# A hybrid recurrence, sparse attention and S5 trunk: one-engine steps and a new order between the weight chunks

## The reference

```python
h = rms_norm(x, norm_g) * (1.0 + scale) + shift
proj = h @ w_in
ya = hgrn2_mixer(hg_q, hg_f, hg_i, lb, hg_onorm_g) * jax.nn.silu(hg_g)
yb = dsa_mixer(at_q, at_k, at_v, ix_q, ix_k, ix_w, positions, at_qnorm_g, at_knorm_g) * jax.nn.silu(at_g)
yc = s5_mixer(s5_u, s5_a_re, ..., s5_glu_w, s5_glu_b) * jax.nn.silu(s5_g)
yd = jnp.einsum('bsnw,nwd->bsnd', jnp.stack([ya, yb, yc], axis=2), w_branch)
merged = jnp.einsum('bsnd,bsnd->bsd', jax.nn.sigmoid(merge_g).reshape(B, S, 3, D), yd)
x = x + gate * (merged @ w_out)
```

## Time and profile before

| | |
|---|---|
| time, median of 3 runs | 1408.55 us (1406.85 to 1410.6) |
| the profiled execution | 1403.91 us, span 1402.1 us |
| mean granted clock of TensorE | 0.955 |
| PE, DVE, ACT, POOL busy | 1290.5, 857.0, 501.4, 488.6 us |
| idle time of PE in the span | 111.6 us |
| HBM | 99 GB/s over the span |

### The profile page before, as it was taken

The page is one execution under the profiler, slowest core; times in us unless marked ns, Lnnn a source line. Parts: engine busy times, 40 slices in busy tenths (PEclk is TensorE's granted clock), DMA queues, the critical chain, the costliest instruction groups (busy, mean ns, idle before and its releaser), DMA issues.

```text
span 1402.1 us, 16539 instructions
## 1 busy us (share of the span) xinstructions
PE 1290.5 (92%) x6240; PEld 1039.1 (74%) x6240; DVE 857.0 (61%) x1396; ACT 501.4 (36%) x774; POOL 488.6 (35%) x344
## 2 busy tenths in 40 slices
PE   7899899789997999989989999988899799999997
PEld 4687787666776877878756877866767588888886
DVE  5775595687647745884464656947865576533241
ACT  5253213443325342333232431143425353333331
POOL 1253222333343323644404432322324332245451
PEclk9999999799997999999989999999999989899999
DMA  9332210032122225562435221110411213344322
GB/s 357 129 135 61 60 61 31 15 137 74 61 90 54 76 77 179 190 243 88 160 123 213 90 61 60 58 34 17 149 61 45 90 55 88 84 155 151 97 69 76
DMA packets 64176, 142.05 MB, mean 101 GB/s; under 512 B 31200, under 2 KB 31328, under 8 KB 63328
## 3 DMA queue, kind: packets, MB, share of 16 engines
q1 hardware_dynamic: 63040, 138.89, 30.2%
q10 hardware_dynamic: 1056, 2.10, 0.4%
HBM read 128.12 MB, written 10.49 MB: 99 GB/s over the span
## 4 chain that ended last, share of the span: by engine, by line
PE 64%; DVE 13%; ACT 8%; SPq 5%; DMA 4%; issue 4%; POOL 1%; DVEq 0%; ACTq 0%
PE bank L1665 16%; PE bank L1666 16%; PE bank L1667 16%; PE bank L1852 4%; DMA raw<-in_wfull 3%; SPq L696 2%; SPq L723 2%; PE bank L1837 2%; SPq L687 1%; PE bank L1921 1%; PE bank L1814 1%; PE bank L1677 1%; ACT w_hi L785 1%; DVE ada L1118 1%; PE bank L1824 1%
## 5 line engine op out<-in xcount | busy, mean ns | idle before, releaser
L756 POOL TENSOR_TENSOR w_lo<-raw,w_hi 128x512 fp32r<-128x512 f32 (+1 forms) x170 | 244.1, 1436 | 893.1 <-ACT w_hi L785 893.1
L1665 PE MATMUL bank<-h_hi,w_hi 128*128 128x512 f32 x896 | 366.0, 408 | 2.3 <-POOL w_lo L757 2.3
L1666 PE MATMUL bank<-h_lo,w_hi 128*128 128x512 f32 x896 | 351.7, 393 | 0.0
L1667 PE MATMUL bank<-h_hi,w_lo 128*128 128x512 f32 x896 | 351.5, 392 | 0.0
L785 ACT ACTIVATE w_hi<-raw 128x1024 fp32r<-128x1024 f32 (+2 forms) x170 | 178.9, 1055 | 300.0 <-PE bank L1667 156.5
L757 POOL TENSOR_TENSOR w_lo<-raw,w_hi 128x512 fp32r<-128x512 f32 (+2 forms) x170 | 252.5, 1486 | 0.0
L1665 PEld LDWEIGHTS bank<-h_hi,w_hi 128*128 128x128 f32 x896 | 170.5, 190 | 45.8 <-issue 8.9
L1666 PEld LDWEIGHTS bank<-h_lo,w_hi 128*128 128x128 f32 x896 | 170.2, 190 | 39.7 <-issue 5.5
L1667 PEld LDWEIGHTS bank<-h_hi,w_lo 128*128 128x128 f32 x896 | 169.9, 190 | 36.6
L1665 PE MATMUL bank<-w_hi,h_hi 128*128 128x512 f32 (+1 forms) x256 | 98.8, 386 | 10.1 <-POOL w_lo L757 4.6
L1666 PE MATMUL bank<-w_lo,h_hi 128*128 128x512 f32 (+1 forms) x256 | 96.5, 377 | 0.0
(11 more groups left out here) (275 smaller groups left out, 1826.4 us busy)
## 6 DMA issues: line engine op xcount, KB each, us to landing
raw<-in_wfull SPq DMA_DIRECT2D x178, 512.0 KB, 3.7
arena<-in_wada SPq DMA_DIRECT2D x40, 512.0 KB, 5.4
x_scratch<-xm SPq DMA_DIRECT2D x2, 2048.0 KB, 8.2
arena<-x_scratch SPq DMA_DIRECT2D x2, 2048.0 KB, 9.4
arena<-in_x SPq DMA_DIRECT2D x4, 512.0 KB, 6.0
arena<-in_s5m SPq DMA_DIRECT2D x2, 1024.0 KB, 4.9
u_scratch<-arena ACTq DMA_DIRECT2D x2, 1024.0 KB, 4.3
arena<-u_scratch SPq DMA_DIRECT2D x64, 32.0 KB, 1.9
```

Source lines behind the costliest of these rows:

```text
L756: nc.gpsimd.tensor_tensor(lo[:, :half], raw_chunk(n)[:, :half], hi[:, :half].bitcast(F32), ALU.subtract)
L1665: mm(out_, a_hi, b_hi, start=first, stop=False)
L1666: mm(out_, a_hi, b_lo, start=False, stop=False)
L1667: return mm(out_, a_lo, b_hi, start=False, stop=last)
```

## The change

The step list from the `kvi` chunks to `wb1` is written anew, and several steps are cut into parts so that each can stand elsewhere.

- Part 9 of the recurrence becomes 9 (states) and 10 (outputs), the old 10 becomes 11 (sum of squares) and 12 (the last DVE step).
- `att(b, ...)` has four parts: logits and exponentials, division, transposes, products.
- The gates leave the chunk's step: `gate(name, j, 0)` and `gate(name, j, 1)`. ACT computes silu instead of sigmoid, and DVE does one multiply instead of two.
- Top keys of block 1 run in rounds of their own (`top1`), those of blocks 2 and 3 in `top`; the work tile lies elsewhere. The indexer goes from block 1 to block 3.
- Squares and sums of q and k are made by ACT as it empties the banks; `kn` normalises k right after its chunk, and k is rotated in the indexer stage. `qs` scales q. The rotations' scratch is now a region of its own, and their waits for the gates are gone.
- SP's code is unchanged, but it walks the new list: `tab(0, 0)` now stands ahead of the last `su` chunk.

```diff
@@ schedule()
+        def top1(*rounds):
+            return [("topk", l, (1,), r) for r in rounds]
+
         def top(*rounds):
-            return [("topk", l, r) for r in rounds]
-        def att(b, part):
-            return [("att", l, b, part)]
+            return [("topk", l, (2, 3), r) for r in rounds]
+
+        def att(b, *parts):
+            return [("att", l, b, part) for part in parts]
+
+        def gate(name, j, *parts):
+            return [("gate", l, name, j, part) for part in parts]
 
         def s5(j, *parts):
             return [("s5", l, j, part) for part in parts]
@@ -117,29 +123,27 @@
-        steps += tm("kvi", 0) + rope("iq0") + tm("kvi", 1) + rope("iq1") + tm("kvi", 2) + rope("ik")
...
-        steps += cm("hq", 1, 0) + hg(0, 2) + idx(2, 7) + idx(1, 0, 1, 2) + cm("hq", 1, 1) + hg(1, 0) + idx(1, 3, 4, 5, 6, 7)
...
-        steps += cm("hg", 0, 0) + hg(1, 8) + cm("hg", 0, 1) + hg(1, 9) + rope("k")
-        steps += cm("hg", 1, 0) + hg(1, 10) + rope("q0") + cm("hg", 1, 1) + rope("q1") + [("par", l)]
...
-        steps += cm("su", 0, 0) + att(3, 0) + cm("su", 0, 1) + cm("su", 1, 0) + att(3, 1) + cm("su", 1, 1) + [("s5u", l)]
-        steps += tab(0, 0, 1) + cm("ag", 0, 0) + tab(0, 2) + cm("ag", 0, 1) + s5(0, 1) + tab(0, 3) + tab(1, 0) + cm("ag", 1, 0)
...
+        steps += rope("iq0") + tm("kvi", 0) + tm("kvi", 1) + tm("kvi", 2) + rope("iq1") + rope("ik") + rope("kn")
+        steps += cm("hf", 0, 0) + tr("iqT2", "ikT") + [("s5l", l, 1)] + tr("iqT1") + cm("hf", 0, 1) + cm("hq", 0, 0) + idx(1, 0, 1, 2)
+        steps += tr("iqT3") + idx(1, 3) + cm("hq", 0, 1) + idx(1, 4, 5, 6, 7) + hg(0, 0) + cm("hf", 1, 0) + rope("k") + idx(2, 0, 1, 2)
+        steps += hg(0, 1) + tr("kT") + top1(0) + cm("hf", 1, 1) + idx(2, 3, 4, 5, 6) + cm("hq", 1, 0) + hg(0, 2) + top1(1, 2) + idx(2, 7)
+        steps += idx(3, 0) + cm("hq", 1, 1) + idx(3, 1) + hg(0, 3) + idx(3, 2, 3) + hg(1, 0) + idx(3, 4, 5, 6) + hg(1, 1) + top1(3, 4)
+        steps += tm("hv", 0) + hg(0, 4) + hg(1, 2) + idx(3, 7) + top1(5) + tm("hv", 1) + tm("hv", 2) + top1(6, 7, 8) + hg(1, 3)
+        steps += tm("hv", 3) + top1(9, 10, 11) + hg(0, 5) + hg(1, 4) + hg(0, 6) + top(0) + tm("q", 0) + hg(1, 5) + hg(0, 7)
+        steps += tm("q", 1) + hg(0, 8) + hg(1, 6) + tm("q", 2) + top1(12, 13, 14) + top(1) + tm("q", 3) + hg(1, 7) + top(2) + rope("qn")
+        steps += top1(15) + hg(0, 9) + cm("hg", 0, 0) + hg(0, 10) + hg(1, 8) + hg(0, 11) + rope("qs") + hg(0, 12)
+        steps += cm("hg", 0, 1) + gate("hg", 0, 0) + rope("q0") + hg(1, 9) + gate("hg", 0, 1) + cm("hg", 1, 0) + hg(1, 10, 11) + rope("q1")
+        steps += hg(1, 12) + cm("hg", 1, 1) + top(3, 4, 5) + tr("qT0") + gate("hg", 1, 0, 1) + cm("mg0", 0, 0) + tr("qT3", "qT1") + top(6)
+        steps += tr("qT2") + cm("mg0", 0, 1) + att(0, 0, 1) + cm("wb0", 0) + att(0, 2) + top(7) + att(1, 0) + cm("mg0", 1, 0) + top(8, 9)
+        steps += att(0, 3) + [("par", l)] + att(1, 1) + cm("mg0", 1, 1) + cm("wb0", 1) + att(1, 2) + cm("mg0", 2, 0) + top(10, 11, 12)
+        steps += att(1, 3) + top(13, 14, 15) + cm("mg0", 2, 1) + cm("wb0", 2) + att(2, 0) + cm("mg0", 3) + att(2, 1, 2)
+        steps += cm("wb0", 3) + cm("su", 0, 0) + att(3, 0) + cm("su", 0, 1) + att(3, 1) + cm("su", 1, 0) + [("s5b", l)] + tab(0, 0)
+        steps += att(2, 3) + att(3, 2) + tab(0, 1) + att(3, 3) + cm("su", 1, 1) + [("s5u", l)] + tab(0, 2) + cm("ag", 0) + gate("ag", 0, 0, 1)
+        steps += s5(0, 1) + tab(0, 3) + cm("ag", 1, 0) + tab(1, 0) + s5(0, 2) + tab(1, 1) + cm("ag", 1, 1) + s5(0, 3) + tab(1, 2)
+        steps += cm("mg1", 0, 0) + gate("ag", 1, 0, 1) + tab(2, 0) + s5(1, 1) + cm("mg1", 0, 1) + s5(0, 4) + tab(1, 3) + s5(1, 2) + tab(2, 1)
+        steps += cm("wb1", 0) + s5(1, 3) + cm("mg1", 1, 0) + gelu(0, 0) + s5(2, 1) + cm("mg1", 1, 1) + tab(3, 0) + s5(1, 4) + tab(2, 2, 3)
+        steps += s5(2, 2) + tab(3, 1) + cm("wb1", 1) + s5(2, 3) + gelu(0, 1) + gelu(1, 0) + cm("mg1", 2, 0) + s5(3, 1)
+        steps += cm("mg1", 2, 1) + tab(3, 2, 3) + s5(2, 4) + s5(3, 2) + cm("wb1", 2) + gelu(1, 1)
...
@@ Banks
+                if part < 12:
+                    banks = take(2)
...
-    "att": lambda s: range(HEADS) if s[3] == 0 else range(HEADS, HEADS + s[2] + 2),
+    "att": lambda s: (range(HEADS), (), range(HEADS, HEADS + s[2] + 1), (HEADS + s[2] + 1,))[s[3]],
...
-        rope = prod
+        rope = region(4096, 2, S)
...
@@ scalar (evacuation of the kvi and q chunks)
+                            sums["k"] = act_mark(nc.scalar.activation(
+                                k_t[:, t * HD:(t + 1) * HD], src[:, 0:HD], ACT.Square, accum_out=stat[:, 16 + t:17 + t]))
...
+                            for h in range(HEADS if name == "q" else 0):
+                                at = slice(h * HD, (h + 1) * HD)
+                                sums["q"] = act_mark(nc.scalar.activation(
+                                    q_t[:, t, at], src[:, at], ACT.Square, accum_out=stat[:, 4 * t + h:4 * t + h + 1]))
...
@@ scalar (kn, qn)
+                    which = step[2][0]
+                    at = stat[:, 0:16] if which == "q" else stat[:, 16:20]
+                    act.wait_ge(act_step, sums[which])
+                    then_wait(nc.scalar.activation(at, at, ACT.Ln, scale=1.0 / HD, bias=eps))
+                    nc.scalar.activation(at, at, ACT.Exp, scale=-0.5).then_inc(qk_norm[which], 1)
...
@@ scalar (gates)
-                        nc.scalar.activation(sig[:, n % 2], src[:], ACT.Sigmoid).then_inc(
-                            read((step, i)) if name[0] == "m" else sig_ready, 1)
...
+                        nc.scalar.activation(sig[:, n % 2], src[:], ACT.Sigmoid if name[0] == "m" else ACT.Silu
+                                             ).then_inc(read((step, i)), 1)
+                if kind == "gate" and step[4] == 0:
...
+                        act.wait_ge(prod_ready, n + 1)
...
+                        nc.scalar.activation(y_hi[:, 2 * j + i], prod[:, n % 2], ACT.Copy).then_inc(y_hi_done, 1)
@@ vector (norms)
-                        then_wait(v.tensor_tensor(rope[:, t % 2], tmb[:, t], tmb[:, t], ALU.mult))
-                        mark(v.tensor_reduce(stat[:, 4 * t:4 * t + 4], r4, AX.X, ALU.add))
-                    after(steps[0])
-                    k4 = rope[:, 0].rearrange("p (h d) -> p h d", h=NT)
-                    then_wait(v.tensor_tensor(k4, kv[:, :, 0:HD], kv[:, :, 0:HD], ALU.mult))
-                    v.tensor_reduce(stat[:, 16:20], k4, AX.X, ALU.add).then_inc(ssq_ready, 1)
-                    dve.wait_ge(ssq_ready, l + 1)
@@ vector (top keys)
-                    r = step[2]
+                    _, _, rows, r = step
                     blocks = []
-                    for b in range(1, NT):
+                    for b in rows:
...
+                    for (acc, _, wk, top), b in zip(blocks, rows):
+                        after(replaced[b])
+                        found.append(mark(v.max(top, wk if r else acc)))
+                    for (acc, _, wk, top), b, n in zip(blocks, rows, found):
                         after(n)
-                        found.append(mark(v.max(top, wk if r else acc)))
@@ vector (gates)
+                if kind == "gate":
+                    _, _, name, j, part = step
...
+                        if part:
+                            dve.wait_ge(y_hi_done, n + 1)
+                            v.tensor_tensor(y_lo[:, k], prod[:, n % 2], y_hi[:, k].bitcast(F32), ALU.subtract
+                                            ).then_inc(y_done, 1)
+                            continue
...
-                        v.tensor_tensor(prod[:, n % 2], src[:], sig[:, sig_no(l, name, k) % 2], ALU.mult
-                                        ).then_inc(read((step, i)), 1)
-                        wait_read(dve, (step, i))
...
-                        v.tensor_tensor(prod[:, n % 2], prod[:, n % 2], pre, ALU.mult).then_inc(prod_ready, 1)
...
-                        dve.wait_ge(y_hi_done, n + 1)
-                        v.tensor_tensor(y_lo[:, k], prod[:, n % 2], y_hi[:, k].bitcast(F32), ALU.subtract
-                                        ).then_inc(y_done, 1)
+                        v.tensor_tensor(prod[:, n % 2], sig[:, sig_no(l, name, k) % 2], pre, ALU.mult).then_inc(prod_ready, 1)
```

More of the change, by code:

```diff
@@ L888, in _ @@
                                              ).then_inc(exp_ready, 1)
-                if kind == "att" and step[3] == 1:
+                if kind == "att" and step[3] == 2:
                     b, key = step[2], step[:3]
@@ L893, in _ @@
                         nc.scalar.activation(p_t[:, s_], src[:], ACT.Copy).then_inc(read((key, HEADS + s_)), 1)
+                if kind == "att" and step[3] == 3:
+                    b, key = step[2], step[:3]
                     src = wait_full(act, (key, HEADS + b + 1))
@@ L1248, in s5_turned @@
                 wait_read(dve, (key, 6))
+            replaced = {}
             for step in STEPS:
@@ L1326, in _ @@
                     dve.wait_ge(rope_tab, 2)
```

(26 more changed lines are left out.)

142 lines of the change are left out of this document (62 added, 80 removed).

## The result

The changed kernel takes 1342.8 us, the median of 4 runs (1338.8 to 1345.0), where the kernel before takes 1408.1 us (4 runs, 1406.9 to 1410.6) on the same chip. The ratio is 0.9547, 95% interval 0.9523 to 0.9571: 65 us faster. The forecast of 1365 was 22 us too high. 1342.8 is in the band of the rival "almost all is won", 1337 to 1350, and outside the forecast's own 1352 to 1378.

A forecast was written before the change was run, and what follows sets the result against it. PE bounds the kernel, so only its pauses and low clock can be won: 23.3 us of pauses, 13.6 of clock and 6.6 of small waits off 1402.1 give 1358.6, the program 1360.4, plus 4.6 for the runs' median: 1365, range 1342 to 1393.

The forecast's parts named there:

- almost all is won: Rival, chance 0.13: clean indexer stage and S5 entries losing half win 18 us of pauses and 10 of clock more, 1337 to 1350.
- The norms; keys early; attention: Waits at state products (8.7 us), query transposes (9.9) and softmax transposes (6.2) go; ikT's late rotation costs 2.2.
- HGRN output: PE's 10.8 us wait there falls to 5.0, and 2.2 of new pauses come at hg(0,11) and hg(1,11).
- Indexer: Index products awaiting two banks cost 7.6 us where 6.0 were; three parts following each other cost 3.5.
- S5 entry: First S5 steps: no gain expected, as SP's loads set the weights' landing; 19 us of 19.4 remain.
- S5 rounds: ACT's long wait behind SP's small copies stays; y copy ahead of the sine table cuts pauses from 4.8 to 3.0 us.
- two short windows a layer: Short half-clock windows, apart from those at S5, expected to remain after the change: 6.8 us in all.
- whose cause I do not see: Half-clock loss of 6.5 us in layer 1, at 1205 to 1226 us, counted as remaining.
- the rival that rested on it: Rival, chance 0.03: a table switch costs twice its row, delaying logarithm, exponential and silu by 7.7 us in all, 1373.
- The clock takes it back: Rival, chance 0.12: some 22 short pauses in the two layers each bring a 1.2 GHz window, 1.7 us lost, 1389.
- The signs named under "wrong": Over 3 us wait at L1888 or ikT, PE wait behind q copies, over 120 us half clock, or S5-round weight waits.
- Slower, by the weight stream: Rival, chance 0.06: in eight S5 rounds SP's 24 small copies delay the next weights; at 7 us a round, 1421.

The follow-up runs named there:

- e3_old_order: The new one-engine parts (squares and sums on ACT, silu, separate gate steps) in the step order of the kernel before: 1392.7 us, ratio 0.9911 to the kernel before.
- e11_old_s5_order: The changed kernel with the old step order from behind su(1,1) to the end of the S5 rounds: 1345.4 us, ratio 0.9561 to the kernel before.

## Why the prediction was right, and where it wasn't

**What bounds the kernel.** Right: PE's work stayed, and the gain is 41.7 us of pauses and 21.1 of clock. Forecast were 29.9 (23.3 and 6.6 of small waits) and 13.6. The missing 19.3 us of span are 11.8 of pauses and 7.5 of clock. The 6.6 had no row under them; the other idle time fell by 5.1, so that term was a guess that came near.

**The norms; keys early; attention.** The 8.7, 9.9 and 6.2 us fell to 0 as said. Two steps under it were wrong. A square with its sum was put at 0.35 us; ACT's timeline shows a pitch of 0.25 to 0.27, since the read of the sum lies under the next square:

```profile
226.78 0.28 ACT L872 ACTIVATE arena<-bank 128x128 f32<-128x128 f32 x1 [4.13 <-PE bank L1674]
226.96 0.19 ACT L872 ACTIVATION_READ_ACCUMULATOR arena<-bank 128x1 f32 x1
227.05 0.27 ACT L872 ACTIVATE arena<-bank 128x128 f32<-128x128 f32 x1
```

That left ikT's rotation 1.4 us early and not 1.1 late: 2.2 us forecast, 0 measured. The squares cost 0.26 us a layer in the wait before hf(0,0) (L868), which the sum hadn't. And that the squares are free on ACT holds by the order alone: in e3_old_order 16 of them, 4.0 us at this pitch, stand ahead of the normalisation of head pair 0, and PE waits 4.2 us a layer.

**HGRN output.** The walk was right in kind: q0 stands ahead of hg(1,9) on DVE, and PE waits 1.4 us where 1.6 were forecast. Head pair 0, put at 0.9, had no wait. 2.8 instead of 5.0, and 1.6 instead of 2.2 for hg(0,11) and hg(1,11).

**Indexer.** Forecast 7.6 and 3.5, measured 2.4 at the index products (L1821, two lines) and 3.8 at the parts (L1860): 6.2 instead of 11.1. The mis-sized term is the section with no chunk in it: the two banks cost 2.0 us a layer and not 3.8.

**S5 entry.** The key step, that SP's loads and not PE set the landing, is what the trace and e11_old_s5_order show. "No gain" was too strong: 19.4 became 13.8, where I left 19.0. In the walk PE's 13.8 us were exact (377.07 to 390.79). The chunk landed 16.6 us after su(1,1), not 18.0: from the end of SP's loads to ACT's split 3.7 us passed, where the earlier trace rows had 5.1. That row is of layer 0; in layer 1 of the same trace it was 3.8, and I priced both layers by the slower one. POOL's halves took 1.26 and not 1.4. So PE went on at 20.3 instead of 22.0. With 0.8 at s5(0,2) the entry costs 13.8 instead of 19.0.

**S5 rounds.** "That stays" was right for ACT's block and too kind to its effect: 3.0 forecast, 4.8 measured, and at another place. I walked the path y save, states, swap, and missed that the block delays the copies of s5(3,1), whose bank s5(2,4) takes.

**The pauses together.** 13.8 + 2.8 + 1.6 + 6.2 + 4.8 = 29.2 us instead of 42.5. The fall in the other idle time is 41.7 - 36.6 = 5.1: small waits of 7.7 us ended, and by the balance 2.6 came.

**The clock.** Left were 22.9 us by the forecast. The half-clock stretches of the changed stages in the profiled run are 393.4 to 400.3, 1052.2 to 1062.4 and 1147.8 to 1161.4, with 2.9, 5.7 and 13.6 us of PE work: half of it is 11.1. In the kernel before, the same stages had 75.3 us of PE work at half clock, half of it 37.6, where I counted 36.5. So these stages won 26.5 us by the clock; the untouched ones lost 2.7 (16.6 us of such work became 22.0), and the 21.1 that PE's busy time shows are 2.7 less than the balance, for which I have no row. The "two short windows a layer" for the indexer's waits, 6.8 us, don't exist: 18 pauses of 0.2 to 1.4 us lie in the stages before the S5 entries, and no stretch. The entries cost 1.5 and 2.8 instead of 4.8 each, as much of a stretch covers the pause itself. The 6.5 us "whose cause I do not see" measured 6.8; their cause in the changed kernel is the pause at s5(2,4), shown by taking it away. For the kernel before, whose pause just ahead of 1211 us was 0.8 us, I only infer it from the place.

**Tables.** Four loads were added in all (55 before, 59 after), not four a layer. The Trainium skill (ScalarE: Activation LUTs, What ACT_TABLE_LOAD costs) gives some 2.66 us for a switch; here again the next operation starts as the load of 1.28 us ends, and the rival that rested on it didn't come:

```profile
481.99 1.28 ACT L1029 ACT_TABLE_LOAD   x1
483.28 0.63 ACT L1029 ACTIVATE arena<-arena 128x512 f32<-128x512 f32 x1
```

**Rivals.** "Almost all is won" asked for a clean indexer stage and half the S5 entries. Neither came whole: 6.2 us in the indexer, 13.8 of 19.4 at the entries. Its time came nevertheless, by several terms each a little better. My waits were nearly all too long, and I gave the side to which they erred 0.13. "The clock takes it back", by short pauses, is refuted for those of the first stages; of the S5 rounds it holds, where it costs 6.8 us at a place. The signs named under "wrong" did not come: the longest wait at L1897 is 1.4 us, none is left before ikT, and the stretches at half clock come to 58 us and not 120. "Slower, by the weight stream" had the right mechanism, SP's copies ahead of the weights, but PE waited for ACT's copies and not for weights, 2 to 3 us a layer.

## What to carry to other kernels

When an engine waits for a transfer in program order, ask what of its queue another engine needs next: here a look ahead of three chunks instead of two put PSUM copies behind a 16 us wait, and taking it back, together with one move in SP's queue, won 36 us after the whole reordering had won 65. Judge one-engine parts in the order that they are to run in: moved to ACT, the norms' work was worth some 15 us in the new order and, by the lists of waits, only moved a wait in the old one. Value a pause by the clock behind it as well, read from a stretch at its place and not from its length.
